# A two-layer decoder trunk on one core: order of the x loads, linear-head states in portions, first output block closed early

## The reference

```python
for l in range(DEPTH):                       # DEPTH = 2
    h = rms_norm(x, attn_norm[l])
    x = x + token_mix(h, ...)                # one input projection, three groups of heads, one output projection
    h = rms_norm(x, mlp_norm[l])
    x = x + squared_relu_mlp(h, w_up[l], w_down[l])   # square(relu(h @ w_up)) @ w_down, D_FF = 4096
```

```python
state_inc = einsum('bnhcd,bnhcv->bnhdv', k_end, vc)          # increments, one per chunk
state = dec[..., None] * state + inc                         # scan over 8 chunks
o = o_intra + einsum('bnhcd,bnhdv->bnhcv', q_dec, s_prev)    # output
o_gla = rms_norm(o, gla_out_norm) * silu(g_gate)
```

## Time and profile before

| what | us |
|---|---|
| median of 3 runs | 1304.08 (1303.95 to 1306.27) |
| profiled execution, its own time | 1305.61 |
| its span (first to last instruction) | 1303.9 |
| PE busy | 1255.1 (96%) |
| DVE busy | 773.8 (59%) |
| ACT busy | 540.4 (41%) |
| POOL busy | 247.1 (19%) |

### The profile page before, as it was taken

One profiled execution on the slowest core, in us unless ns is written; L12 is line 12 of the kernel. 1 busy time (PEld: TensorE's weight loads), 2 busy tenths in 40 slices (PEclk: granted clock), 3 DMA queues, 4 the chain that ended last, 5 costly groups with the idle time before them and its releaser, 6 DMA issues.

```text
span 1303.9 us, 19103 instructions
## 1 busy us (share of the span) xinstructions
PE 1255.1 (96%) x5916; PEld 983.1 (75%) x5916; DVE 773.8 (59%) x1240; ACT 540.4 (41%) x871; POOL 247.1 (19%) x157
## 2 busy tenths in 40 slices
PE   4999999899999999999999999988999999999997
PEld 3856777578888888888877568765888888888886
DVE  4579866734454454444766888575445445445458
ACT  4474435834413314224436643376442242231343
POOL 4022340011020020110531324200201201102016
PEclk9999999999999999999999999999999999999999
DMA  5312220023222222222232112200233223222223
GB/s 200 101 49 65 65 98 1 2 65 110 97 96 97 97 97 97 97 97 97 97 99 81 56 59 82 65 2 2 97 125 97 97 96 97 96 96 98 96 98 129
DMA packets 31023, 110.46 MB, mean 85 GB/s; under 512 B 3568, under 2 KB 3568, under 8 KB 30960
## 3 DMA queue, kind: packets, MB, share of 16 engines
q1 hardware_dynamic: 29088, 103.82, 24.0%
q0 software_dynamic: 576, 3.76, 0.8%
q10 hardware_dynamic: 1296, 2.12, 0.5%
HBM read 107.59 MB, written 2.10 MB: 84 GB/s over the span
## 4 chain that ended last, share of the span: by engine, by line
PE 89%; DVE 3%; ACT 3%; issue 3%; POOL 1%; DMA 1%; DVEq 0%; ACTq 0%; SPq 0%; POOLq 0%
PE bank L824 18%; PE bank L823 18%; PE bank L822 18%; PE bank L477 6%; PE bank L479 6%; PE bank L478 6%; PE bank L511 2%; PE bank L500 2%; PE bank L498 2%; PE bank L499 2%; PE bank L709 1%; PE bank L736 1%; PE bank L721 1%; PE bank L693 1%; POOL lnb L410 1%
## 5 line engine op out<-in xcount | busy, mean ns | idle before, releaser
L877 ACT ACTIVATE wh<-raw 128x1024 fp32r<-128x1024 f32 x194 | 204.8, 1056 | 397.3 <-PE bank L824 239.0
L1165 DVE TENSOR_TENSOR wl<-raw,wh 128x1024 fp32r<-128x1024 f32 x158 | 247.2, 1565 | 102.6 <-ACT wh L877 95.1
L822 PE MATMUL bank<-hh,wl 128*128 128x512 f32 x512 | 200.0, 391 | 0.0
L822 PE MATMUL bank<-xmh,wl 128*128 128x512 f32 x512 | 199.3, 389 | 0.0
L824 PE MATMUL bank<-hl,wh 128*128 128x512 f32 x512 | 199.2, 389 | 0.0
L824 PE MATMUL bank<-xml,wh 128*128 128x512 f32 x512 | 199.2, 389 | 0.0
L823 PE MATMUL bank<-xmh,wh 128*128 128x512 f32 x512 | 199.2, 389 | 0.0
L823 PE MATMUL bank<-hh,wh 128*128 128x512 f32 x512 | 199.2, 389 | 0.0
L445 POOL TENSOR_TENSOR x<-x,rsb 128x512 f32<-128x512 f32 x64 | 84.6, 1322 | 580.3 <-DVE rsb L1555 580.3
L477 PE MATMUL bank<-xgh,wl 128*128 128x512 f32 x368 | 152.7, 415 | 23.5 <-DVE xgl L1174 18.3
L1544 DVE TENSOR_TENSOR sqb<-tf 128x512 f32<-128x512 f32 x64 | 44.3, 693 | 181.3 <-ACT hh L1136 181.3
(11 more groups left out here) (190 smaller groups left out, 1747.6 us busy)
## 6 DMA issues: line engine op xcount, KB each, us to landing
raw<-in_stream SPq DMA_DIRECT2D x194, 512.0 KB, 3.3
x<-in_x ACTq DMA_DIRECT2D x8, 256.0 KB, 12.5
out_y<-x SPq DMA_DIRECT2D x8, 256.0 KB, 4.3
par<-in_params POOLq DMA_DIRECT2D x2, 916.0 KB, 4.9
con<-in_consts POOLq DMA_DIRECT2D x1, 944.5 KB, 9.2
par<-in_params POOLq DMA_DIRECT2D x1, 896.0 KB, 11.4
par<-in_params ACTq DMA_DIRECT2D x1, 20.0 KB, 1.8
```

The costliest lines, as they stand in the source:

```text
L822: pe.matmul(B.t[s][:], wl[:, s, n_block(k)], src_h[:, k], start=(k == 0), stop=False)
L877: act.activation(wh[:, s], raw[:, s], ACT.Copy).then_inc(hi_ready.sem, 1)
L1165: vec.tensor_tensor(wl[:, s], raw[:, s], wh[:, s], ALU.subtract).then_inc(lo_ready.sem, 1)
```

## The change

1. **Start.** x comes in four loads of two planes: ACT issues planes 0-1 and 4-5, POOL issues 2-3 and 6-7. POOL issues `con` and `par` only when planes 6-7 have landed. ACT splits block 0, then makes all `xgh` ahead of block 1's split; squares of planes 0 to 3 are made between, those of 4 to 7 after it. The sums of squares of the first layer move from POOL to DVE. DVE waits for `con` and `par` only in unit 2's evacuation, and for `rb` (the norm factor) only at the evacuation of `iq0`, behind a low part instead of ahead of it.
2. **Units 0 to 2, both layers.** `total("xstat", 0)` runs behind unit 1 and the transposes behind unit 2. `small` goes to bank 2.
3. **Linear heads.** The increments of the second pair of heads are made behind `turn(0)`, into banks 7 and 1 (6 and 7 before); DVE's states go in four portions, the first two behind `normalise(0)`, the others in steps j = 0 and 1. `stat(gst h)` stands ahead of `gla_out` and `weigh_pair` in its step.
4. **End of attention.** ACT makes the factor of `aost2` behind the last two copies of transposes, not ahead of them. `out1` gets two planes, then `out0` its last, then `out1` the other six (seven, one, one before).

The core of the diff, without the helpers that only rename:

```diff
 USES = (
-    [("iq0", 0), ("xstat", 6), ("iq1", 1), ("rcol", 7), ("small", 0),
+    [("iq0", 0), ("iq1", 1), ("xstat", 6), ("small", 2), ("rcol", 7),
...
-    + [("inc00", 4), ("inc01", 5), ("inc10", 6), ("inc11", 7)]
+    + [("inc00", 4), ("inc01", 5), ("inc10", 7), ("inc11", 1)]
...
         def _(pool):
...
+            for d in (2, 6):
+                pool.dma_start(x[:, d:d + 2], x_in[:, d:d + 2]).then_inc(x_loaded[d // 2], 16)
+            pool.wait_ge(x_loaded[3], 16)
             pool.dma_start(con[:], consts).then_inc(const_loaded, 16)
             pool.dma_start(par[:, W_GATE:N_PAR], params[0][:, W_GATE:N_PAR]).then_inc(par_loaded, 16)
-            for k in range(KB):
-                sum_square(0, 0, k)
...
                 unit(0, before=x_part)
-                total("xstat", 0)
                 pe.wait_ge(*dn_freed[1].at(l, -1))
                 alone(pe)
                 unit(1)
+                total("xstat", 0)
+                unit(2)
                 pe.wait_ge(*rb_ready.at(l, 0))
...
-                unit(2)
                 token_units(l, 3, DV_BLOCKS, DVW, "dv")
...
-                    if h == 0:
-                        pe.wait_ge(*B.freed(l, "inc11"))
+                    if h % 2 == 0:
+                        pe.wait_ge(*B.freed(l, f"inc{h // 2}1"))
...
+                increments(0)
                 for j in range(N_ATT + LAG):
...
                         turn(j)
+                    if j == 0:
+                        increments(1)
+                    if j in STAT_SLOT:
+                        h = STAT_SLOT[j]
+                        stat(l, f"gst{h}", ones[:], sq_of(f"gst{h}"))
                     if j in OUT_SLOT:
                         gla_out(OUT_SLOT[j])
                     if j >= LAG and (j - LAG) % 2 == 1:
                         weigh_pair(j - LAG - 1)
...
-                    if j in STAT_SLOT:
-                        h = STAT_SLOT[j]
-                        stat(l, f"gst{h}", ones[:], sq_of(f"gst{h}"))
...
-                first_out(1, 0, KB - 1)
+                first_out(1, 0, 2)
                 first_out(0, KB - 1, KB)
-                first_out(1, KB - 1, KB)
+                first_out(1, 2, KB)
...
             split(0, 1)
+            act.wait_ge(gains_loaded, 16)
+            for k in range(0, KB, 2):
+                act.wait_ge(x_loaded[k // 2], 16)
+                gained_high(k, xgh, G_ATTN)
+                gained_high(k + 1, xgh, G_ATTN)
+                if k in (0, 2):
+                    squared(0, 0, k)
+                    squared(0, 0, k + 1)
             split(1, 1)
-            act.wait_ge(gains_loaded, 16)
-            for k in range(KB):
-                act.wait_ge(x_loaded[k], 16)
-                gained(0, 0, k, xgh, G_ATTN)
+            for k in range(4, KB):
+                squared(0, 0, k)
...
-                    if j % PAIR == LAG + 4 and j > PAIR:
+                    if j % PAIR == LAG + 4 and PAIR < j < N_ATT - 2:
                         factor(f"aost{j // PAIR - 1}", DH)
...
+                factor("aost2", DH)
                 mix_high(6, MIXED[6])
```

62 lines of the change are left out of this document (41 added, 21 removed).

## The result

The changed kernel takes 1285.48 us (1284.52 to 1289.46, 5 runs) against 1305.66 us (1303.95 to 1308.55, 5 runs) of the kernel before: a ratio of 0.9853, 95% interval 0.9833 to 0.9874. Its profiled execution has a span of 1283.8 us where the one before had 1303.9, so 20.1 us went; the predicted sum was 22.8.

What follows compares the result with a forecast made beforehand. PE, busy 1255.1 of 1303.9 us, was taken as the bound, with at most 48.8 idle. Gains of 8.1 + 6.0 + 1.0 + 7.7 = 22.8 from 1305.6 gave 1282.8; the median lying 1.5 lower, 1281 was forecast, range 1276 to 1289.

Steps and rivals of the forecast that it cites:

- The start: First layer up to unit 3: it starts at 30.6 us instead of 38.63, gain 8.1 us, bounds 6.0 and 9.3.
- DVE's pace: Start: DVE sets the pace, 10.3 us of its work up to the second low part; unit 1 at 18.2.
- the 12.36 us behind it: Start: units 1 and 2, the total and the transposes cost PE 12.36 us, so unit 3 starts at 30.6.
- The choice of 0 for POOL's clearing beside DVE: Start: POOL's clearing of `gqp` within DVE's chain costs between 0 and 1.0 us; taken as 0.
- transfers to be off the path: Start: queues share equally, planes 0-1 and 2-3 there at 7.2 us, everything at about 11, so no transfer delays.
- the prediction's own sign: Start: all `xgl` near 0.75 us, unit 1 at 18 to 19; wrong if `xgl` stays 1.77 or ACT waits for a transfer.
- The start of attention: Both layers: PE's waits of 1.44 and 0.70 go, plus 1.64 of clock in the first; gain 6.0 us, bounds 3.0 and 7.
- The rival that ACT and DVE give this gain back later: Attention, 205 to 250 us: ACT and DVE set the pace, so the 6.0 is lost; total gain 16.8, 1287; chance 0.07.
- The statistics ahead of the outputs: Linear heads: waits 1.3 added, 1.2 removed, ACT's exponentials held up less; +0.5 a layer, +1.0, bounds -2.5 and +4.
- The half clock in the middle: Rival at attention's waits: gaps move and the clock falls at the new ones; gain 15.8, 1288; chance 0.17.
- The end of attention: Both layers: 0.95, 2.41 and 1.7 of half clock go, 1.2 is added; 3.86 a layer, 7.7, bounds 4.2 and 8.5.
- The new wait: End of attention: PE waits about 1.2 us ahead of `out0`'s last plane, with only the statistic and two planes as cover.

Runs made afterwards that it cites:

- states as before: Changed kernel with only the state portions undone (all 56 increments ahead of the loop, all states ahead of normalise(0)): 1289.98 us, 0.9875.
- late statistics: Changed kernel with only the linear heads' statistics put back behind outputs and weighting: 1285.02 us, 0.9833.
- the end as before: Changed kernel with only the end of attention undone (factor ahead of the last copies, seven planes of out1 ahead of out0's last): 1295.21 us, 0.9909.
- the start alone: Changed kernel with state portions, early statistics and end-of-attention edits undone, start and units 0 to 2 as changed: 1296.37 us, 0.9926.
- constants in front: Changed kernel with POOL issuing constants and parameters (1.84 MB) ahead of its two loads of x, without the wait: 1292.67 us, 0.9905.

## Why the prediction was right, and by how much it was off

**The result** of 1285.5 lies in the range (1276 to 1289) and 4.5 above the 1281 forecast. The sum was 22.8 where 20.1 was measured, which is 2.7 of the 4.5. The rest is the kernel before: its median was 1305.66 beside the changed kernel, where the prediction started from 1304.1.

**The start**: 8.1 predicted, 8.3 measured. DVE's pace, unit 1 at 18.2 (18.05), the 12.36 us behind it (12.27) and the total without a wait all held. The steps are borne out singly: with the total in its old place 3.2 us go, with POOL's sums 1.9. The choice of 0 for POOL's clearing beside DVE was right.

The closeness of the number is in part luck. The prediction took 10.3 us of DVE's work up to unit 1 at 18.2, so a start at 7.9. It had seen that ACT issues fewer loads, but not how much that gives: DVE starts at 6.57, 1.3 us sooner. Against that it took transfers to be off the path, with planes 2-3 there at 7.2 us at a third of the rate for each queue. They came at 10.57, because POOL's queue had moved 0.20 MB by 7.1 us and the others 0.62 each, and DVE stood idle for 1.05 us in all, 0.86 of it for planes 2-3. The two errors nearly cancel. By the prediction's own sign ("wrong if `xgl` stays at 1.77 or ACT waits for a transfer") this step was wrong: ACT waits 1.09 us for planes 2-3. The totals of 1.52 and 3.02 MB, from which equal shares were read, say nothing of how queues share. The size has a spread, too: with the late quickening of PE the start is worth 7.2 to 7.7.

On the queues: the second pair can be used at 10.57 us when it leads POOL's queue, at 11.19 behind the first pair in ACT's, and at 16.44 behind 1.84 MB of constants and parameters in POOL's. So what stands in front in a queue delays what is behind it. The Trainium skill (DMA: Bandwidth & Descriptors, Queues, rings and completion order) has the DMA engines take packets in turn from the queues that hold work. From 7.1 us on the trace agrees roughly (0.58, 0.45 and 0.43 MB); before, it agrees only if POOL's queue did not always hold work, which no run shows.

**The start of attention**: 6.0 predicted, 6.2 measured. Both waits went, in both layers, and the half clock of the first layer with them. The states as before bring them back with 1.35 and 0.70 us. The rival that ACT and DVE give this gain back later did not come: the 56.06 us of the middle before, less the wait of 0.95 and plus the 0.45 of the early statistics, make 55.56, and at full clock it takes 55.62.

**The statistics ahead of the outputs: the mis-sized term.** Predicted +1.0, measured -0.9 by the segments, and -1.0 between runs of equal clock (changed kernel 1284.34 to 1284.58, late statistics 1283.37 and 1283.49). The waits were foreseen almost exactly: 1.3 added (0.60, 0.38, 0.18), 1.2 removed (0.77, 0.34). What failed is the sentence after them, "so I give this part +0.5 a layer": no wait stood behind that half microsecond, only the thought that ACT's factor would be less in the way. It is 1.9 of the 2.7 that are missing. The waits of the two orders come out even, but the segment does not, and no run shows where the rest of the 0.45 a layer goes.

**The half clock in the middle** was held to be a rival (1288, the clock falling at new gaps), which took 3.5 off the statistics' term and 3.5 off the end's. It came in part: 1.4 us in the first layer of the profiled run, 2.6 in both layers of another. The rival's picture, a low clock behind short waits close together, fits what was seen, though waits alike to the hundredth also passed without a fall. Its place was neither of the two named, but a pair of waits that had stood there before without a fall (231.40 and 233.27 us in the trace of before, 0.77 and 0.69 us).

**The end of attention**: 7.7 predicted, 8.1 measured (3.1 twice, and 0.95 twice, which lies in the middle segment). The 2.41 went and the 0.95 went. The new wait was 0.73 and not 1.2. The chain from the statistic (254.92) to the last plane (257.65) takes 2.73 us, as in the earlier trace rows; but the statistic and the two planes lie over more of it than the 1.62 counted, 1.84 us from start to start, which leaves 0.9, and the profile counts 0.16 of that as the tail of the last matmul. With a third plane there is no wait. The 1.7 us of half clock a layer, counted as gained if the new gap left the clock alone, are a chance also on the other side: they were there in the profile of before and with the end as before, not in that of the start alone. So some 3.1 of the 8.1 us measured here depend on which execution of the kernel before was profiled.

Against the 22.8, then, there stand +0.4 at the end, +0.2 each at the two starts, -1.9 from the statistics and -1.4 from the clock: 20.3, and 20.1 were measured.

**A faster version.** The changed kernel with three planes of `out1` ahead of `out0`'s last plane takes 1283.13 us, 0.9829 (0.9812 to 0.9847); the changed kernel has 0.9853 to 0.9870 in its three sets, with intervals that overlap. By segments its gain is 1.3 us; that its medians lie further apart is the clock, which all its five runs kept.

## What to carry to other kernels

Before an engine's slow instruction is counted as its cost, look at what the other engine does beside it, at what the engine ahead of it is busy issuing, and at which queue carries the first data that everything waits for: here the constants ahead of two pairs of planes would have cost 5.9 us, three times what the moved sums were worth. When a wait is taken away by giving its cover to something else, price both sides from rows and put nothing on top. Separate in every trace the segments at full clock from those at half: differences of one or two microseconds were settled here only by segments at equal clock. And repeat the same kernel before reading such a difference from one profile: here two profiles of one kernel differ by 0.8 us at the start and 1.2 in the middle of the second layer.

## What the runs showed of the hardware

- **A slow pace of a PE that was idle, at a granted clock of 1.00.** Unit 0's matmuls start 0.43 us apart from 8.8 us on, after an idle start; they go over to 0.23 us at 13.65 us in one run of the changed kernel and at 17.21 in another, with the same waits ahead (8.8 and 0.49), and between 12.16 and 17.80 over the eight profiles with this start. The stretches from 8 to 22 us show a granted clock of 1.00 in both. With a wait of 6.8 us in between (constants in front) it was 20.8. The pace of matmuls, not the clock's row, tells it.
- **Half clock behind short waits, and not each time**: 1.4 us lost at one place, 1.6 behind a wait of 2.41, 3.7 up to head 2's scores when the low stretch lasted some 10 us (states as before, 188 to 199: 14.84 us less the 11.16 of the second layer), and 1.0 more behind them (56.35 against 55.39).
- **DVE and POOL slow each other** in sums and differences of two SBUF tiles (1.77 against 0.75 us for `xgl`, 2.30 against 1.22 for a low part, 1.46 to 2.08 against 1.28 for POOL's sum), while POOL's clearing of a tile beside `xgl` left it at 0.75.
- **POOL's queue starts slowly.** Of three queues with work issued to them from 0.9 to 2.7 us, those of ACT and SP had moved 0.62 MB each by 7.1 us and POOL's 0.20 (0.19 to 0.21 in three other profiles with loads of x at the head of POOL's queue, 0.30 with the constants in front). In packets these were 48 against SP's 167; in the kernel before, where POOL's queue carried only constants and parameters, 55 larger ones (0.42 MB) against 191. From 7.1 to 10.57 us POOL's moved the most, 0.58 MB.
- **One execution of 4892.51 us** in a set whose others took 1284.34 to 1288.34. Its matmuls are all slow, from the first one on, at a granted clock of 1.00:

```profile
L828 PE MATMUL bank<-hh,wh 128*128 128x512 f32 x512 | 563.3, 1100 | 0.0
```

The same group in the changed kernel's page:

```profile
L828 PE MATMUL bank<-hh,wh 128*128 128x512 f32 x512 | 199.2, 389 | 0.0
```

The other engines worked at their usual speed (DVE busy 773.8 us, ACT 545.1). It is left out of the ratio; nothing in its trace says what it was.
